# Sixteen of 31 taps as stacked diagonals in the second depthwise convolution, 24 in its last tile

## The reference

```python
def depthwise_conv(y, w, b):
    # 31 taps, one weight per channel and tap
    out = lax.conv_general_dilated(y, w[:, None, :], window_strides=(1,), padding=((15, 15),), feature_group_count=C)
    return out + b

def conv_branch(h, w_in, dw, db, ln_g, ln_b, w_out):
    a, b, gate = jnp.split(h @ w_in, 3, axis=-1)
    y = a * jax.nn.sigmoid(b)
    y = depthwise_conv(y, dw, db)
    y = jax.nn.silu(layernorm(y, ln_g, ln_b))
    return (y * jax.nn.silu(gate)) @ w_out
```

## Time and profile before

| | |
|---|---|
| median of 3 runs | 2968.45 us (2968.0 to 2968.6) |
| the profiled execution | 2965.42 us |
| its span, first to last instruction | 2963.6 us |
| PE busy in the span | 2630.6 us (89%), 28836 records |
| DVE busy | 1514.9 us (51%), 2663 |
| ACT busy | 1134.5 us (38%), 1779 |
| POOL busy | 764.7 us (26%), 438 |
| mean granted clock of PE | 0.946 of 2.4 GHz |

### The profile page before, as it was taken

One profiled execution on the slowest core, in us unless ns is written; L12 is line 12 of the kernel. 1 busy time (PEld: TensorE's weight loads), 2 busy tenths in 40 slices (PEclk: granted clock), 3 DMA queues, 4 the chain that ended last, 5 costly groups with the idle time before them and its releaser, 6 DMA issues. The chain is left out here.

```text
span 2963.6 us, 66747 instructions
## 1 busy us (share of the span) xinstructions
PE 2630.6 (89%) x28836; PEld 2005.7 (68%) x28836; DVE 1514.9 (51%) x2663; ACT 1134.5 (38%) x1779; POOL 764.7 (26%) x438
## 2 busy tenths in 40 slices
PE   7898899979899996888888888879999999898987
PEld 5676587747677785776677666658678655476745
DVE  4634578883652214545554544334550166525995
ACT  4533332242453333444444443233432344323333
POOL 2322200002212125544544441212223200032201
PEclk9999899989889897999999999889999999999998
DMA  4224434333434531111111100541322200044431
GB/s 151 78 63 136 141 112 113 81 122 117 155 146 153 186 117 51 41 41 52 42 32 49 50 10 25 184 156 53 125 58 78 71 1 1 22 161 138 139 88 57
DMA packets 83663, 266.38 MB, mean 90 GB/s; under 512 B 11824, under 2 KB 12848, under 8 KB 82992
## 3 DMA queue, kind: packets, MB, share of 16 engines
q1 hardware_dynamic: 74160, 236.97, 25.0%
q10 hardware_dynamic: 9216, 25.17, 2.1%
HBM read 203.04 MB, written 36.70 MB: 81 GB/s over the span
## 5 line engine op out<-in xcount | busy, mean ns | idle before, releaser
L373 PE MATMUL ps<-h_parts_conv,w_parts_one 128*128 128x512 f32 x3168 | 580.2, 344 | 13.2 <-DVE h_parts_conv L359 11.3
L373 PEld LDWEIGHTS ps<-h_parts_conv,w_parts_one 128*128 128x128 f32 x3168 | 496.0, 192 | 101.6 <-DVE h_parts_conv L359 17.8
L373 PE MATMUL ps<-scratch_scan 64*64 64x64 f32 (+1 forms) x15936 | 377.5, 237 | 85.0 <-issue 46.5
L373 PEld LDWEIGHTS ps<-scratch_scan 64*64 64x64 f32 x15936 | 339.8, 139 | 129.1 <-issue 85.2
L441 POOL TENSOR_TENSOR w_parts_rwkv_out<-ring,w_parts_rwkv_out 128x1024 fp32r<-128x1024 f32 x80 | 191.1, 2391 | 787.7 <-ACT w_parts_rwkv_out L370 787.7
L441 POOL TENSOR_TENSOR w_parts_one<-ring,w_parts_one 128x1024 fp32r<-128x1024 f32 x82 | 205.9, 2512 | 690.0 <-ACT w_parts_one L370 689.9
L370 ACT ACTIVATE scratch_scan<-ps 128x384 f32<-128x384 f32 x560 | 241.1, 492 | 367.0 <-PE ps L373 224.3
L367 DVE SCALAR_TENSOR_TENSOR scratch_conv<-scratch_conv,vec 128x256 f32<-128x256 f32 (+1 forms) x656 | 330.3, 579 | 0.2
L373 PE MATMUL ps<-h_parts_attn,w_parts_rwkv_out 128*128 128x512 f32 (+1 forms) x1536 | 326.1, 371 | 0.0
L373 PEld LDWEIGHTS ps<-h_parts_attn,w_parts_rwkv_out 128*128 128x128 f32 x1536 | 262.9, 188 | 56.1 <-issue 8.0
L370 ACT ACTIVATE w_parts_rwkv_out<-ring 128x1024 fp32r<-128x1024 f32 x104 | 109.6, 1056 | 371.5 <-PE ps L373 343.5
(11 more groups left out here) (218 smaller groups left out, 3368.9 us busy)
## 6 DMA issues: line engine op xcount, KB each, us to landing
ring<-in_weights SPq DMA_DIRECT2D x311, 512.0 KB, 3.9
rwkv_spill<-scratch_conv ACTq DMA_DIRECT2D x64, 384.0 KB, 2.3
stream<-rwkv_spill SPq DMA_DIRECT2D x64, 384.0 KB, 3.9
scratch_conv<-scratch_conv SPq DMA_DIRECT2D x128, 103.1 KB, 2.2
scratch_conv<-scratch_conv SPq DMA_DIRECT2D x128, 67.4 KB, 2.0
x_spill<-stream SPq DMA_DIRECT2D x2, 3072.0 KB, 11.9
y_spill<-scratch_scan SPq DMA_DIRECT2D x8, 384.0 KB, 4.1
scratch_rwkv_out<-y_spill SPq DMA_DIRECT2D x8, 384.0 KB, 6.2
```

The source lines that it names most:

```text
L373: return nc.tensor.matmul(o, l, r, start=start, stop=stop)
```

## The change

The number of groups becomes a matter of the layer and tile: `NGRP = 3, 4`, with 6 for tile 7 of the second convolution. The first convolution keeps 3 groups (12 taps on PE, 19 on DVE). In the second, tiles 0 to 6 have 4 groups (16 taps on PE, 15 on DVE), tile 7 has 6 (24 on PE, 7 on DVE). Tile 7's diagonals use both DIAG buffers, so POOL waits for the PE taps of tile 6 before it writes them, not of tile 5. DVE's taps are cut in thirds of the tile's own count. The stacked copies and their 16 DMAs stay as they are. The table of vectors grows by 24 columns of 128 (496 to 520 for the taps' weights).

```diff
-NGRP = 3
-SHARE = TAPS - 4 * NGRP
+NGRP = 3, 4
+NGRP_LAST = 6
+SHARE = tuple(TAPS - 4 * n for n in NGRP)
...
-            DIAG = take(2, NGRP * 4, 32)
+            DIAG = take(2, NGRP[j_] * 4, 32)
...
-            dve_taps = [(t, n) for t in range(TAPS) for n in range(2) if t < SHARE]
-            cut = [len(dve_taps) * s // 3 for s in range(4)]
+            def last(m):
+                return j_ == 1 and m == DT - 1
+
+            def groups(m):
+                return NGRP_LAST if last(m) else NGRP[j_]
+
+            def share(m):
+                return TAPS - 4 * groups(m)
+
+            def diagonals(m):
+                return DIAG.rearrange("p a b n -> p (a b) n") if last(m) else DIAG[:, m % 2]
...
                 if m >= 2:
-                    g.wait_ge(pe_taps, past + m - 1)
+                    g.wait_ge(pe_taps, past + m - (not last(m)))
+                n = 4 * groups(m)
...
-                nc.gpsimd.tensor_tensor(DIAG[:, m % 2], ident, w, ALU.mult).then_inc(diag_ready, 1)
+                nc.gpsimd.tensor_tensor(diagonals(m)[:, 0:n], ident, w.rearrange("p (q o) -> p q o", o=1).broadcast_to([P, n, 32]),
+                                        ALU.mult).then_inc(diag_ready, 1)
...
-                for q in range(NGRP):
+                for q in range(groups(m)):
                     for a, b, c in halves:
-                        y = yoff[c] + SHARE + 4 * q - PAD
+                        y = yoff[c] + share(m) + 4 * q - PAD
                         for j in range(4):
-                            last = mm(TAPS_PS[32 * j:32 * j + 32, a:b], DIAG[:, m % 2, 4 * q + j, :], BST[:, j, y:y + b - a],
-                                      q == 0, q == NGRP - 1)
+                            last = mm(TAPS_PS[32 * j:32 * j + 32, a:b], diagonals(m)[:, 4 * q + j, :], BST[:, j, y:y + b - a],
+                                      q == 0, q == groups(m) - 1)
...
-                for j in range(cut[s], cut[s + 1]):
+                dve_taps = [(t, n) for t in range(share(m)) for n in range(2)]
+                for j in range(len(dve_taps) * s // 3, len(dve_taps) * (s + 1) // 3):
```

More of the change, by code:

```diff
@@ L44, in vector_table @@
              ("b_ple_gate", 8), ("final_norm_w", 8), ("c_2", 8), ("c_ctx_2", 8),
-             ("norm_g_2", 32), ("mod_b_2", 96), ("conv_dw_2", 2 * SHARE * 8), ("conv_st_2", 2 * NGRP * 4 * 8), ("conv_db_2", 16),
+             ("norm_g_2", 32), ("mod_b_2", 96), ("conv_dw_2", sum(SHARE) * 8), ("conv_st_2", sum(NGRP) * 4 * 8), ("conv_last_2", NGRP_LAST * 4),
[1 row of a table added]
              ("conv_ln_g_2", 16), ("conv_ln_b_2", 16), ("rwkv_mu_2", 48), ("rwkv_w0_2", 16),
@@ L1235, in conv_layer @@
             pieces = [(0, TX, yoff[0]), (TX, TT, yoff[1])] if nh == 2 else [(0, TX // 2, yoff[0]), (TX // 2, TX, yoff[0] + TX // 2)]
-            dve_taps = [(t, n) for t in range(TAPS) for n in range(2) if t < SHARE]
-            cut = [len(dve_taps) * s // 3 for s in range(4)]
+            def last(m):
[6 more added lines that the diff above has]
+                return DIAG.rearrange("p a b n -> p (a b) n") if last(m) else DIAG[:, m % 2]
             used_y = XW + CW if nh == 2 else XW
             def tap_weight(m, t):
-                return V("conv_dw_2", (j_ * SHARE + t) * DT + m)
+                return V("conv_dw_2", (j_ * SHARE[0] + t) * DT + m)
             def build_diagonals(g, m):
                 if m >= 2:
-                    g.wait_ge(pe_taps, past + m - 1)
-                ident = C("ident4").rearrange("p (o n) -> p o n", o=1).broadcast_to([P, NGRP * 4, 32])
-                w = V("conv_st_2", (j_ * DT + m) * NGRP * 4, NGRP * 4).rearrange("p (q o) -> p q o", o=1).broadcast_to([P, NGRP * 4, 32])
-                nc.gpsimd.tensor_tensor(DIAG[:, m % 2], ident, w, ALU.mult).then_inc(diag_ready, 1)
+                    g.wait_ge(pe_taps, past + m - (not last(m)))
+                n = 4 * groups(m)
+                ident = C("ident4").rearrange("p (o n) -> p o n", o=1).broadcast_to([P, n, 32])
+                w = V("conv_last_2", 0, n) if last(m) else V("conv_st_2", j_ * DT * 4 * NGRP[0] + m * n, n)
+                nc.gpsimd.tensor_tensor(diagonals(m)[:, 0:n], ident, w.rearrange("p (q o) -> p q o", o=1).broadcast_to([P, n, 32]),
+                                        ALU.mult).then_inc(diag_ready, 1)
             def stack_shifts(sp, m):
@@ L3022, in pack @@
     dw = a["conv_dw_2"].reshape(2, TAPS, DT, 4, 32)
-    st = dw[:, SHARE:].reshape(2, NGRP, 4, DT, 4, 32)
-    a["conv_st_2"] = st.transpose(0, 3, 1, 4, 2, 5)
-    a["conv_dw_2"] = dw[:, :SHARE]
+    st = [dw[l, SHARE[l]:].reshape(NGRP[l], 4, DT, 4, 32).transpose(2, 0, 3, 1, 4).reshape(-1, P) for l in range(2)]
+    last = dw[1, TAPS - 4 * NGRP_LAST:, DT - 1].reshape(NGRP_LAST, 4, 4, 32)
+    a["conv_st_2"] = np.concatenate(st)
+    a["conv_last_2"] = last.transpose(0, 2, 1, 3)
+    a["conv_dw_2"] = np.concatenate([dw[l, :SHARE[l]].reshape(-1, P) for l in range(2)])
     vectors = np.concatenate([a[n].reshape(-1, P).T for n in VT], 1)
```

## The result

The changed kernel takes 2978.19 us (median of 19 runs) against 2968.45 of the kernel before, 1.0034 times as long, with a 95% interval of 1.0025 to 1.0043: it is slower by about 10 us. The runs spread wider than the three first shown, 2969 to 2988 for the changed kernel and 2965 to 2977 for the one before. The forecast was 2970.1, no change that could be measured, with a range to 2974.0. The profiled execution took 2975.56, its span 2973.8.

The account below looks back on a forecast made before the run. It took PE (19.40 us a round) and DVE (20.28) as near equal limits, with two branches ending nearly together. The stage's end came 1.6 us later; 2968.45 + 1.6 = 2970.1 us, range 2966.3 to 2974.0.

Parts of the forecast that it names:

- Two near equal limits in the middle, 19.40 on PE and 20.28 on DVE: Second convolution's tile rounds before the change: PE needs 19.40 us, DVE 20.28; PE waits 2.1 us in all seven.
- A group costs PE 0.87 us, so the rounds are 20.27: Tiles 0 to 6: one more group adds 8 PE records, 0.87 us, lengthening PE's round from 19.40 to 20.27 us.
- DVE's saving is worth nothing: Second convolution: DVE's round falls to about 17.1 us, and it ends tile 7's taps nearly 13 us sooner, unused.
- SP starts the last copies when PE's taps of tile 6 end, at the same time as before: Tile 7: SP's wait on YP becomes one on BST; start about 2855.75 in the trace, 2855.69 before.
- 11.51 us from there to PE's start: Tile 7: from SP's start on the copies to PE's taps takes 11.51 us as before, so PE starts at 2867.26.
- PE's 48 records in 6.75 us, with 2.88 us at the low clock: Tile 7's taps on PE: 5.31 us at full clock plus 1.44 for 2.88 us at the 1.2 GHz level.
- The last diagonals come in time; DVE loses one instruction to them: POOL's 128x768 build for tile 7 ends between 2857.4 and 2864.9, before the copies at 2867.26; costed at nothing.
- the third rival: Tile 7's last diagonals come late: DVE keeps POOL out until 2863.7, PE waits, +7.2 us, 2975.7 us; chance 0.03.
- The sum: Second convolution's end: the block ends at 2881.47 against 2879.86, 1.6 us later, added to the median 2968.45.
- The larger table of vectors is 12 KB more in one load, for which I take nothing.: Load of the table of vectors: 12 KB more in one load, put at no time.
- a sign for rounds above 20.5 us: PE's rounds in the second convolution: above 20.5 us would mean a wait the prediction didn't have.
- the low way: Rival for tile 7: the clock stays low through all 48 PE records, +3.9 us more, 2974.0 us; chance 0.07.

Follow-up runs that it names:

- b_sums_first: Kernel before, 3 groups in all tiles, with PE's sums of tiles 0 to 6 ahead of the last tile's taps: 2966.12 against 2966.99 us, single run.
- b_pad24: Kernel before with 24 unused columns in the table of vectors, so the split weights lie 96 bytes higher: 1.0014, 2972.25 against 2969.65 us.
- a_same_place: Changed kernel with a scratch tensor cut by 24 columns, so split weights and inputs lie as in the kernel before: 1.0012, 2971.67 us.
- b_last6: Changed kernel, addresses as before the change, with 3 groups in tiles 0 to 6 and 6 in the last: 2971.76 against 2966.56 us, single run.
- b_low: Kernel before with the split inputs laid right above the split weights, except in the attention layer: 0.9992, 2962.64 against 2966.75 us.
- a_sums_first: Changed kernel, addresses as before the change, with PE's sums of tiles 0 to 6 ahead of the last tile's taps: 0.9993 of the kernel before.
- a_sums_low: a_sums_first with the split inputs placed as in b_low: 0.9975 of the kernel before, 2959.73 against 2966.75 us.
- a_last4: Changed kernel, addresses as before the change, with 4 groups in the last tile too: 2970.45 against 2966.56 us, single run.

## Why the prediction was wrong

The measured time lies 8.1 us above the forecast. Two terms of the sum that were sized too small make 1.9 us of it; the rest comes from a term that the prediction put at nothing.

- *Two near equal limits in the middle, 19.40 on PE and 20.28 on DVE.* Right. `b_sums_first` and `b_pad24` still have the waits on DVE, the changed kernel has none.
- *A group costs PE 0.87 us, so the rounds are 20.27.* Right: 20.27 in `a_same_place`.
- *DVE's saving is worth nothing.* Right; it waits 10.6 us for PE at the end.
- *SP starts the last copies when PE's taps of tile 6 end, at the same time as before.* Right: 164.0 us from the stage's first gain instruction in `a_same_place` (2693.71 to 2857.72) and before (2691.66 to 2855.69).
- *11.51 us from there to PE's start.* Mis-sized: 12.10 us. SP's issues took 10.6 us or more and not 10.0 whenever they started together with POOL's build (10.56, 10.60, 10.63, 10.83, 10.92 and 11.10), and 10.00 or 10.01 when they did not, in `b_last6` and in `b_low` among others. That POOL is the cause was not tried.
- *PE's 48 records in 6.75 us, with 2.88 us at the low clock.* Mis-sized: 8.08 us in `a_same_place`, 7.12 in the changed kernel. The windows of `a_same_place`, PE alone (the third number from the right is the granted clock), show the low level for some 5.5 us of work; with 1.2 of 2.4 GHz half of it is lost:

```profile
2869.82:2875.40 5.58, 5.58 (x28) 0.50 0.93 356
2875.40:2877.90 2.50, 2.50 (x24) 0.98 0.07 30
```

- *The last diagonals come in time; DVE loses one instruction to them.* Right. In `a_same_place` the build takes 3.58 us and ends at 2861.31, 8.5 us ahead of PE's start. POOL didn't have to wait for DVE's last taps, as the third rival needs: it ended 1.3 us behind DVE's ten instructions of tile 6. DVE's first TENSOR_SCALAR was the one held up.
- *The sum.* 1.6 us for the change; in the place of before it measures 3.4. The difference is 0.6 for the copies and 1.3 for the clock. With this alone the time would have stayed in the range: 2971.67 us, between 2966.3 and 2974.0. The size of the clock's part was chance as far as the runs tell: the same 48 records took 6.89 to 8.08 us in those that have the sums behind them.
- *"The larger table of vectors is 12 KB more in one load, for which I take nothing."* This step failed. I priced what the table costs to load and not where it pushes what lies behind it. It moved the split weights against the split inputs by 96 bytes and made some 2500 products 4 ns slower. That would be 10 us; part of it is hidden behind DVE in the second convolution, and the first convolution became faster, so 4 to 5 us are left by `b_pad24`, and 1.5 more in the second convolution, since the change had given the rounds to PE. By the profiles, 3.4 for the change, 5 for the place and 1.5 for both make 9.9 of the 10.2 us of span. The prediction had a sign for rounds above 20.5 us, but read it as a wait: the rounds came at 20.57, and PE waited for nothing.
- *The rivals.* None had the place. The slower one, late diagonals, had the right sign for a cause that didn't occur. The clock did go the low way, by 1.3 of the 3.9 us that I gave to that rival.

Left open: why the distance matters. The runs show that the remainder by 128 bytes doesn't settle it, and two good values; what in the chip makes it so, whether all multiples of 16384 are good, and what sets the pace of the stretches on two widths, they don't show.

## What to carry to other kernels

A change of a table's size is a change of every address behind it: keep the addresses when you compare, or measure the padding by itself. When two branches end together, shortening one shows nothing; look for the order of work on the other and change both. And an engine that idles for a late transfer should be given work that is ready. Here the clock stayed up through the last taps in the two runs that left PE a rest of 0.8 us or less ahead of them (`a_sums_first`, `a_sums_low`), and not in the two that left 2.7.

## What the runs showed of the hardware

A matrix product on 512 columns from split (fp32r) operands, in a stretch of such products alone, took 0.2273 to 0.2333 us at full clock, going with how far the stationary and the moving tensor lie apart in the on-chip memory: 3%. Moving them by 96 bytes made this kernel 4 to 5 us slower. Stretches of 512 and 256 columns by turns took 25.2 or 25.7 us for 144 products, and the distance alone doesn't say which.

A 128x384 build of POOL next to a busy DVE took up to 4.60 us, a 128x512 one of the changed kernel, in a gap of DVE, 1.06. The 768 columns took 3.47. So the durations of POOL in the trace of before were mostly time in which it was kept waiting, and an estimate in proportion to the columns (9.2 us) was far too high. Much of the 3.47 is waiting too: in `a_last4` a build of 512 columns that started at the same point took 3.15.
